# Gated DeltaNet bodies of a decoder layer: GpSimd takes six weight-tile subtractions of each body over from VectorE

## The chip, the cores and the metric

The kernel runs on one NeuronCore of a Trainium2 chip. The metric is the device time of one launch in microseconds (us), taken as the median of several runs. Engines are named PE (TensorE), DVE (VectorE), ACT (ScalarE), POOL (GpSimd) and SP (SyncE, which issues most transfers).

## What is computed

One decoder layer on 256 tokens of width 2048, in float32: a large input projection, two token mixers on its columns (a gated delta rule and a differential attention), a gated merge, an output projection with layer norm, and a SwiGLU feed-forward. Cut to what matters here:

```python
h = x @ w_in[l]                       # q, k, v, z of the delta rule, then the attention's and the gates
qkv = silu(causal_depthwise_conv(concat([q, k, v]), conv_w))
# delta rule, per head and chunk of 64 tokens:
a_mat = where(strict, einsum('cd,sd->cs', k_beta, k) * decay, 0)
sol = triangular_solve(a_mat + eye(64), [v * beta, k_beta * exp(g)], unit_diagonal=True)
...
o_a = rms_norm(o, norm_w) * silu(z)
merged = sigmoid(ga) * (o_a @ w_branch_a) + sigmoid(gb) * (o_b @ w_branch_b)
x = layer_norm(alpha * x + merged @ w_out); ffn = (silu(x @ w_gate) * (x @ w_up)) @ w_down
x = layer_norm(alpha * x + ffn)
```

## The kernel before

Every weight is read once, as a stream of 640 tiles of 128 x 1024 float32 numbers (512 KB), in the order in which they are used. A product in float32 accuracy is made from three passes in the type float32r: SP brings a tile to `raw` (a ring of four buffers), ACT rounds it to `whi` ("hi"), and the remainder `wlo = raw - whi` ("lo") is taken by a subtraction with two inputs in SBUF. PE then multiplies activations by both: 12 products of 128x512 for a tile, `act_hi*whi`, `act_hi*wlo`, `act_lo*whi`.

Order is written out by hand. The stream is cut into bodies of 32 tiles, called slots `s = 0..31` (BODY). In slot `s` PE multiplies tile `s`, while ACT (`split` on line 811) and DVE (`split` on line 1280) prepare tile `s + 3` (AHEAD = 3). Both wait for `tile_used` to reach `n + s`, so they may begin when PE has left tile `s - 1`; DVE waits for `hi_done` too. PE waits before a tile for `hi_done` and `lo_done`, which count the tiles in order (lines 440 and 441), and SP waits for both before it fills a `raw` buffer anew.

The first four bodies (j = 0 to 3, `body(0, ...)` and a loop) multiply the delta rule's k, v, q and z columns of four heads each. Between tiles the engines work at the delta rule itself, each by a list of "mixes" called after the slot's split:

- `dn_conv`: in slots 8, 10, 16, 18, 24 and 26 PE turns two heads of the projection, ACT takes the last tap, and DVE adds three others by six `SCALAR_TENSOR_TENSOR` (line 1405; one input in PSUM, one in SBUF). In the slot after, ACT applies SiLU (line 927).
- `dn_build`: the inverse of the triangular matrix. In slot 15 DVE makes masks of it (`Pm<-AT,masks`, `Tc<-Pm,masks`, `Pc<-Tc`, `Pm<-masks,Tc`). It then grows in five steps, in slots 17, 19, 20, 21 and 22 (GROW, k = 0 to 4). In each, PE waits for `dve_x`, multiplies `B<-Pm,Pc` (64 small products), and DVE makes what the next step needs:

```python
dve.wait_ge(N["pe_x"], 1 + GROWN * j + k + 1)
ch(tt(Pm[:, :, :], Pm[:, :, :], B8[1], ALU.subtract))      # one input in PSUM
ch(V.transpose(Tc[:, :, :], WT))                           # one input
tt(Pc[:, :, :], Tc[:, :, :], rep(masks[:, k + 2, :], 8), ALU.mult).then_inc(N["dve_x"], 1)   # two in SBUF
```

- `dn_scan` (slots 0 to 12 of the next body): the recurrence over chunks.

POOL has only small work in these bodies: `root` (lines 1237 to 1247), twelve instructions of 128x8 that refine a reciprocal root. Its result `rinv` is asked for in slot 13 and used in slot 28. A second root is asked for in slot 6 of the next body. Instructions on POOL and DVE run in the order in which they are written.

Of the kernel before, what the change touches and what calls it, by code (L numbers as in the profile page):

```python
# [18 lines left out]
ALU = mybir.AluOpType  # L19
# [24 lines left out]
CONV_LINKS, BUILD_LINKS, SCAN_LINKS, DA_LINKS = 12, 19, 7, 25  # L44
OT_SLOTS = (12, 14)
O_BLOCKS, V_BLOCKS = 11, 22
O_HI = 29
V_SCALED = (28, 30)
TURN = range(1, 7)
TURN_HI = 8  # L50
GAIN = (11, 13)
# [9 lines left out]
RING = 4  # L61
AHEAD = 3
# [6 lines left out]
BODY = 4 * TPG  # L69
# [32 lines left out]
def build(nc, xT, xrow, weights, w_ab, consts, early, params, lam_in, ln_in, out):  # L102
    ctx = ExitStack()

    def sb(name, shape, dt=F32):
        return ctx.enter_context(nc.sbuf_tensor(name, shape, dt))

    def sem(name):
        return ctx.enter_context(nc.semaphore(name))

    with ctx:
# [33 lines left out]
        raw = sb("raw", [P, RING, TK, NG])  # L145
        whi = sb("whi", [P, RING, TK, NG], F32R)
        wlo = sb("wlo", [P, RING, TK, NG], F32R)
# [44 lines left out]
        def conv_bank(kind, half):  # L192

            return B[1 if kind == 0 and half else 0]
# [9 lines left out]
        def d_(name):  # L204
            a, b = DS[name]
            return dsm[:, a:b]
# [48 lines left out]
        hi_done = sem("hi_done")  # L255
        lo_done = sem("lo_done")
        tile_used = sem("tile_used")
# [972 lines left out]
        @block.gpsimd  # L1230
        def _(pool):
            G = nc.gpsimd
            for n in counted:
                pool.sem_inc(N[n], 1)
            ch = Chain(pool, N["pool_chain"], 1)

            def root(o, x):

                a = half[:, 0:x.shape[1]]
                for i in range(3):  # L1240
                    ch(G.tensor_tensor(a, o, o, ALU.mult))  # L1241
                    ch(G.tensor_tensor(a, a, x, ALU.mult))
                    ch(G.tensor_scalar(a, a, -0.5, 1.5, ALU.mult, ALU.add))  # L1243
                    last = G.tensor_tensor(o, a, o, ALU.mult)
                    if i < 2:
                        ch(last)
                return last

            for j in range(NB + 1):
                if j > 0:  # L1250
                    pool.wait_ge(N["dve_qs"], 1 + j)
                    root(d_("rs"), d_("qs")).then_inc(N["pool_rs"], 1)
                if j < NB:
                    pool.wait_ge(N["dve_ss"], 1 + j + 1)
                    ch(root(d_("rk"), d_("ss")))
                    G.tensor_tensor(d_("rinv"), d_("rk"), d_("ss"), ALU.mult).then_inc(N["pool_rinv"], 1)
            for i in range(HEADS):
                pool.wait_ge(N["dve_os"], 1 + i + 1)
                root(sm[:, 48:50], sm[:, 42:44]).then_inc(N["pool_os"], 1)

        @block.vector
        def _(dve):
            V = nc.vector

            def tt(o, a, b, op):
                return V.tensor_tensor(o, a, b, op)  # L1266
# [6 lines left out]
            def stt(o, a, s, b, op0, op1):  # L1273
                return V.scalar_tensor_tensor(out=o, in0=a, scalar=s, in1=b, op0=op0, op1=op1)  # L1274
# [5 lines left out]
            def split(n, s):  # L1280

                if isinstance(n, int) and n + s + AHEAD >= N_TILES:
                    return
                r = (s + AHEAD) % RING
                dve.wait_ge(hi_done, n + s + AHEAD + 1)
                dve.wait_ge(tile_used, n + s)
                tt(wlo[:, r], raw[:, r], whi[:, r], ALU.subtract).then_inc(lo_done, 1)
# [99 lines left out]
            def dn_conv(j, s):  # L1387
                if s == 4:
                    dve.wait_ge(N["act_tap"], 1 + 6 * j)
                    a0 = PARAM["conv"][0]  # L1390
                    V.tensor_copy(cw[:, :, :, :].rearrange("p k h c -> p (k h c)").unsqueeze(1),
                                  par[:, a0:a0 + NB * 48].rearrange("p (j c) -> p j c", j=NB)
                                  [:, bass.ds(j, 1), :]).then_inc(N["dve_cw"], 1)
                for kind, slots in enumerate(CONV_SLOTS):
                    if s not in slots:
                        continue
                    half = slots.index(s)
                    link = Chain(dve, N["conv_chain"], 1 + CONV_LINKS * j + 2 * (2 * kind + half))
                    dve.wait_ge(N["act_tap"], 1 + 6 * j + 2 * kind + half + 1)
                    for back in range(1, CONV):  # L1400
                        for i in range(2):
                            h = 2 * half + i
                            w = cw[:, kind, h, CONV - 1 - back:CONV - back]
                            dst = cT[:, kind, h, back:SEQ]
                            ins = stt(dst, conv_bank(kind, half)[:, i * SEQ:(i + 1) * SEQ - back], w, dst, ALU.mult, ALU.add)
                        if back == CONV - 1:
                            ins.then_inc(N["dve_conv"], 1)
                        else:
                            link(ins)

            def v_scaled(j, t):
                tt(vr[:, t].rearrange("p h (a x) -> p h a x", x=SB), by_source(vtok).rearrange("p (h t) a x -> p h t a x", t=TOK)[:, :, t],
                   d_("rinv")[:, HB * t:HB * (t + 1)].unsqueeze(2).unsqueeze(3).broadcast_to([P, HB, 4, SB]), ALU.mult
                   ).then_inc(N["dve_v"], 1)

            def dn_build(j, s, ch):
# [54 lines left out]
                if s == V_BLOCKS:  # L1471
                    dve.wait_ge(N["act_silu"], 1 + 3 * j + 2)
                    if not isinstance(j, int):
                        dve.wait_ge(o_kept, 16 * j)
                    V.transpose(stage[:, :, :, :].rearrange("p b q x -> p q b x"),
                                cT[:, 1].rearrange("p h (q b x) -> p (h q) b x", q=TOK, x=SB)).then_inc(N["dve_vS"], 1)
                if s in V_SCALED:
                    if s == V_SCALED[0]:
                        dve.wait_ge(N["pool_rinv"], 1 + j + 1)
                        dve.wait_ge(v_full, 64 * (j + 1))  # L1480
                    v_scaled(j, V_SCALED.index(s))
                if s in (28, 29):
# [56 lines left out]
                    tt(lo(act_a, HB * j, HB, t * P, (t + 1) * P), B4[2 + t],  # L1539
                       hi(act_a, HB * j, HB, t * P, (t + 1) * P), ALU.subtract).then_inc(N["dve_oT"], 1)  # L1540

            def body(n, mixes=()):
                for s in range(BODY):
                    split(n, s)
                    for mix in mixes:
                        mix(s)

            def chained(name, base, fn, j, links, slots=BODY, **more):
                ch = Chain(dve, N[name], 1 + base)
                def run(s):  # L1550
                    fn(j, s, ch, **more)
                    if s == slots - 1:
                        assert ch.n == links, (name, ch.n)
                return run

            body(0, [prologue, chained("build_chain", 0, dn_build, 0, BUILD_LINKS), lambda s: dn_conv(0, s)])
            with dve.Fori(1, NB) as j:
                body(BODY * j, [chained("scan_chain", SCAN_LINKS * (j - 1), dn_scan, j - 1, SCAN_LINKS),
                                chained("build_chain", BUILD_LINKS * j, dn_build, j, BUILD_LINKS),
                                lambda s: dn_conv(j, s)])  # L1560

            def da_mix(j, s, ch):
                if s == 0:
# [43 lines left out]
            def da_turns(j, s, first):  # L1607
                for which, slots in enumerate(DA_TURN_FIRST if first else DA_TURN):
# [11 lines left out]
                    if i == 15:  # L1620
                        ins.then_inc(N["dve_qkT"], 1)

            body(N_DA, [chained("scan_chain", SCAN_LINKS * (NB - 1), dn_scan, NB - 1, SCAN_LINKS,
                                alone=True), lambda s: da_turns(0, s, True)])
            with dve.Fori(1, NB) as j:
# [12 lines left out]
            def turn_blocks(cnt, s, place):  # L1638

                if s == TURN[0]:  # L1640
                    dve.wait_ge(N["dve_m"], 1 + cnt + 1)
                    dve.wait_ge(N["act_mT"], 1 + 2 * cnt)
                if s in TURN:
                    at = 3 * (s - TURN[0])
                    for i in range(at, min(at + 3, 16)):
                        a, b = divmod(i, 4)
                        ins = V.transpose(blocks_out(turned)[b * SB:(b + 1) * SB, :, :, a, :],  # L1647
                                          blocks_in[a * SB:(a + 1) * SB, :, :, b, :])
                    if s == TURN[-1]:
                        ins.then_inc(N["dve_turn"], 1)  # L1650
# [28 lines left out]
            for g in range(3):  # L1679
                for q in range(TPG):  # L1680
                    s = g * TPG + q
# [304 lines left out]
```

## Time and profile before

| | |
|---|---|
| median of 3 runs | 1930.88 us (1929.91 to 1931.75) |
| the profiled execution | 1930.64 us, of it 1928.8 us from first to last instruction |
| PE busy | 1913.5 us (99%) |
| DVE busy | 1330.6 us (69%) |
| ACT busy | 928.9 us (48%) |
| POOL busy | 101.3 us (5%) |
| granted PE clock | 0.998 of full speed |

The busy times are shares of the span. PE's products overlap each other, so its 99% means that it hardly waits, not that it is at its peak.

### The profile page before, as it was taken

The page shows a single profiled execution, that of the slowest core. Times are in us where ns is not written, and L with a number is a line of the kernel's source. Part 1 is how long each engine was busy: PE and PEld are TensorE (multiplying, and loading weights), DVE is VectorE, ACT ScalarE, POOL GpSimd, SP SyncE. Part 2 cuts the span into 40 slices and gives each one's busy share as a digit, 9 for nine tenths or more (in the row PEclk, how much of TensorE's full clock was granted, in tenths as well). Part 3 has the DMA queues.
Part 4 walks back from the last instruction along what each step waited for, and adds up shares of the span by engine and source line. Part 5 has one row for each costly group of instructions (what it writes and reads, how often), then busy time and mean ns, then how long its engine had stood idle before and what let it go on. Part 6 is the DMA issues. An engine that isn't in the chain of part 4 may idle for free.

```text
span 1928.8 us, 31440 instructions
## 1 busy us (share of the span) xinstructions
PE 1913.5 (99%) x10359; PEld 1574.6 (82%) x10359; DVE 1330.6 (69%) x1872; ACT 928.9 (48%) x1308; POOL 101.3 (5%) x296
## 2 busy tenths in 40 slices
PE   9999999999999999999999999999999999999997
PEld 7788888888888888888888887888888888888886
DVE  7868688786757777776566756577675466665656
ACT  5555564554455555545544436544443444443442
POOL 0102020010002121212000000000000000000000
PEclk9999999999999999999999999999999999999999
DMA  7555555564655555555666676565666556666655
GB/s 280 165 166 184 182 172 178 167 187 146 201 171 169 179 168 179 166 182 165 206 194 191 214 248 199 175 195 189 193 196 193 191 194 191 196 192 195 196 187 175
DMA packets 103672, 362.57 MB, mean 188 GB/s; under 512 B 11472, under 2 KB 15376, under 8 KB 103440
## 3 DMA queue, kind: packets, MB, share of 16 engines
q1 hardware_dynamic: 97904, 351.65, 56.7%
q10 hardware_dynamic: 5664, 9.46, 1.5%
q8 instruction: 74, 1.21, 0.3%
q14 instruction: 30, 0.25, 0.0%
HBM read 355.28 MB, written 5.78 MB: 187 GB/s over the span
## 4 chain that ended last, share of the span: by engine, by line
PE 92%; DVE 4%; ACT 2%; issue 1%; DMA 0%; SPq 0%; DVEq 0%; ACTq 0%
PE pg L415 86%; PE B L415 4%; DVE wlo L1266 1%; DVE cT L1274 1%; DVE gates L1274 1%; DVE Pm L1266 1%; DVE AT L1266 1%; ACT QKT L959 0%; PE B L513 0%; DMA raw<-in_weights 0%; ACT whi L809 0%; PE B L666 0%; DVE Tc L1457 0%; PE B L538 0%; PE B L631 0%
## 5 line engine op out<-in xcount | busy, mean ns | idle before, releaser
L1266 DVE TENSOR_TENSOR wlo<-raw,whi 128x1024 fp32r<-128x1024 f32 (+1 forms) x640 | 779.2, 1221 | 470.0 <-ACT whi L809 452.2
L809 ACT ACTIVATE whi<-raw 128x1024 fp32r<-128x1024 f32 (+1 forms) x640 | 674.3, 1057 | 700.9 <-PE pg L415 687.1
L415 PE MATMUL pg<-whi,act_x 128*128 128x512 f32 x2960 | 950.0, 395 | 0.7 <-ACT whi L809 0.7
L415 PEld LDWEIGHTS pg<-whi,act_x 128*128 128x128 f32 x2960 | 555.5, 188 | 123.8 <-issue 7.9
L415 PE MATMUL pg<-wlo,act_x 128*128 128x512 f32 x1480 | 574.8, 390 | 0.0
L415 PE MATMUL pg<-whi,act_a 128*128 128x512 f32 x1632 | 504.9, 389 | 0.5 <-DVE act_a L1266 0.3
L415 PEld LDWEIGHTS pg<-whi,act_a 128*128 128x128 f32 x1632 | 306.3, 188 | 64.9 <-DVE act_a L1266 1.3
L415 PEld LDWEIGHTS pg<-wlo,act_x 128*128 128x128 f32 x1480 | 278.3, 188 | 53.7
L415 PE MATMUL pg<-wlo,act_a 128*128 128x512 f32 x816 | 317.5, 389 | 0.0
L415 PEld LDWEIGHTS pg<-wlo,act_a 128*128 128x128 f32 x816 | 153.2, 188 | 31.6
L415 PE MATMUL pg<-whi,act_b 128*128 128x512 f32 x512 | 158.3, 389 | 0.0
L415 PEld LDWEIGHTS pg<-whi,act_b 128*128 128x128 f32 x512 | 96.1, 188 | 19.9
L415 PE MATMUL pg<-wlo,act_b 128*128 128x512 f32 x256 | 99.6, 389 | 0.0
L1647 DVE STREAM_TRANSPOSE soft<-hraw 32x256 f32<-32x256 f32 x208 | 90.6, 436 | 3.8
L1274 DVE SCALAR_TENSOR_TENSOR cT<-B,cw,cT 128x255 f32<-128x255 f32 (+1 forms) x144 | 62.7, 477 | 5.5 <-ACT cT L922 3.6
L415 PEld LDWEIGHTS pg<-wlo,act_b 128*128 128x128 f32 x256 | 48.0, 188 | 10.1
L1073 ACT ACTIVATE soft<-soft,sm 128x128 f32<-128x128 f32 (+1 forms) x64 | 28.4, 444 | 38.2 <-DVE sm L1270 38.2
L1241 POOL TENSOR_TENSOR half<-dsm 128x8 f32<-128x8 f32 x24 | 14.3, 594 | 437.3 <-DVE dsm L1271 436.0
L900 ACT ACTIVATE hraw<-pg 128x512 f32<-128x512 f32 x40 | 21.7, 594 | 32.2 <-PE pg L415 27.4
L922 ACT ACTIVATE cT<-B,cw 128x256 f32<-128x256 f32 x48 | 20.1, 470 | 32.8 <-PE B L513 31.8
L1243 POOL TENSOR_SCALAR half<-half 128x2 f32<-128x2 f32 (+1 forms) x72 | 33.6, 467 | 6.3
L1241 POOL TENSOR_TENSOR half<-sm 128x2 f32<-128x2 f32 x48 | 11.9, 248 | 357.6 <-DVE sm L1271 355.1
(231 smaller groups left out, 1048.6 us busy)
## 6 DMA issues: line engine op xcount, KB each, us to landing
raw<-in_weights SPq DMA_DIRECT2D x646, 512.0 KB, 4.2
decm<-sums_out ACTq DMA_DIRECT2D x4, 512.0 KB, 4.4
turn_v<-stage ACTq DMA_DIRECT2D x4, 512.0 KB, 2.9
kT<-turn_v ACTq DMA_DIRECT2D x16, 128.0 KB, 2.9
gates<-in_ln_in SPq DMA_DIRECT2D x4, 512.0 KB, 6.0
gates<-in_ln_in SPq DMA_DIRECT2D x1, 2048.0 KB, 8.4
out<-gates SPq DMA_DIRECT2D x8, 256.0 KB, 2.7
turn_o<-stage ACTq DMA_DIRECT2D x3, 512.0 KB, 4.3
```

Source lines behind the costliest of these rows:

```text
L415: return nc.tensor.matmul(o, l, r, start=start, stop=stop)
L809: return nc.scalar.activation(o, i, ACT.Copy, scale=scale)
L900: last = nc.scalar.activation(dst(t), pg[pair][t][:, :], func, scale=scale)
L922: last = nc.scalar.activation(cT[:, kind, h, :], conv_bank(kind, half)[:, i * SEQ:(i + 1) * SEQ], ACT.Copy, scale=cw[:, kind, h, CONV - 1: ...
L1073: last = nc.scalar.activation(pr[:, m, a:b], pr[:, m, a:b], ACT.Exp, bias=sm[:, 28 + i:29 + i], accum_out=sm[:, 32 + i:33 + i])
L1241: ch(G.tensor_tensor(a, o, o, ALU.mult))
L1243: ch(G.tensor_scalar(a, a, -0.5, 1.5, ALU.mult, ALU.add))
L1266: return V.tensor_tensor(o, a, b, op)
L1274: return V.scalar_tensor_tensor(out=o, in0=a, scalar=s, in1=b, op0=op0, op1=op1)
L1647: ins = V.transpose(blocks_out(turned)[b * SB:(b + 1) * SB, :, :, a, :], blocks_in[a * SB:(a + 1) * SB, :, :, b, :])
```

## The change

In each delta-rule body the lo subtractions of slots 16, 18, 20, 22, 24 and 26 (those for tiles 19, 21, 23, 25, 27 and 29) are issued on POOL, behind the `rinv` of that body. Each waits for the hi of its tile, for the lo of the tile before, and for its buffer (`tile_used`). DVE leaves them out. In the slot after each it waits until POOL's lo is counted, and then goes on with the next tile's lo. The lo's of the whole stream stay in order.

```diff
+POOL_LO = (16, 18, 20, 22, 24, 26)
...
                     G.tensor_tensor(d_("rinv"), d_("rk"), d_("ss"), ALU.mult).then_inc(N["pool_rinv"], 1)
+                    for s in POOL_LO:
+                        n = BODY * j + s
+                        r = (s + AHEAD) % RING
+                        pool.wait_ge(hi_done, n + AHEAD + 1)
+                        pool.wait_ge(lo_done, n + AHEAD)
+                        pool.wait_ge(tile_used, n)
+                        G.tensor_tensor(wlo[:, r], raw[:, r], whi[:, r], ALU.subtract).then_inc(lo_done, 1)
...
-            def body(n, mixes=()):
+            def body(n, mixes=(), by_pool=()):
                 for s in range(BODY):
-                    split(n, s)
+                    if s - 1 in by_pool:
+                        dve.wait_ge(lo_done, n + s + AHEAD)
+                    if s not in by_pool:
+                        split(n, s)
                     for mix in mixes:
                         mix(s)
...
-            body(0, [prologue, chained("build_chain", 0, dn_build, 0, BUILD_LINKS), lambda s: dn_conv(0, s)])
+            body(0, [prologue, chained("build_chain", 0, dn_build, 0, BUILD_LINKS), lambda s: dn_conv(0, s)], POOL_LO)
             with dve.Fori(1, NB) as j:
...
-                                lambda s: dn_conv(j, s)])
+                                lambda s: dn_conv(j, s)], POOL_LO)
```

On POOL, between the end of a body's `rinv` (`dsm<-dsm`) and the root of the next body, there stood before:

```order
L1244 TENSOR_TENSOR dsm<-half,dsm 128x8 [waits pool_chain]
L1256 TENSOR_TENSOR dsm<-dsm 128x8 [waits pool_chain]
L1241 TENSOR_TENSOR half<-dsm 128x8 [waits dve_qs]
L1242 TENSOR_TENSOR half<-half,dsm 128x8 [waits pool_chain]
L1243 TENSOR_SCALAR half<-half 128x8 [waits pool_chain]
```

and there stands now:

```order
L1245 TENSOR_TENSOR dsm<-half,dsm 128x8 [waits pool_chain]
L1257 TENSOR_TENSOR dsm<-dsm 128x8 [waits pool_chain]
L1264 TENSOR_TENSOR wlo<-raw,whi 128x1024 [waits tile_used,lo_done,hi_done] x6
L1242 TENSOR_TENSOR half<-dsm 128x8 [waits dve_qs]
L1243 TENSOR_TENSOR half<-half,dsm 128x8 [waits pool_chain]
L1244 TENSOR_SCALAR half<-half 128x8 [waits pool_chain]
```

Six subtractions of 128x1024 have come in behind `rinv`, and nothing else on POOL has moved.

On DVE, slots 15 and 16 of the first body: the end of the mask work, the lo of slot 16, and the first of the six `cT<-B,cw,cT` of the convolution. Before:

```order
L1266 TENSOR_TENSOR Tc<-Pm,masks 128x256 [waits build_chain]
L1444 STREAM_TRANSPOSE Pc<-Tc 128x256 [waits build_chain]
L1266 TENSOR_TENSOR Pm<-masks,Tc 128x8x32
L1266 TENSOR_TENSOR wlo<-raw,whi 128x1024 [waits tile_used,hi_done,build_chain]
L1274 SCALAR_TENSOR_TENSOR cT<-B,cw,cT 128x255 [waits act_tap]
```

Now:

```order
L1274 TENSOR_TENSOR Tc<-Pm,masks 128x256 [waits build_chain]
L1452 STREAM_TRANSPOSE Pc<-Tc 128x256 [waits build_chain]
L1274 TENSOR_TENSOR Pm<-masks,Tc 128x8x32
L1282 SCALAR_TENSOR_TENSOR cT<-B,cw,cT 128x255 [waits act_tap,build_chain]
L1282 SCALAR_TENSOR_TENSOR cT<-B,cw,cT 128x255
```

The convolution now stands directly behind the mask work.

On DVE, slots 19 to 21 of the first body, with the growing steps k = 1 and k = 2 (`Pm<-Pm,B`, `Tc<-Pm`, `Pc<-Tc,masks`). Before:

```order
L1266 TENSOR_TENSOR wlo<-raw,whi 128x1024 [waits tile_used,hi_done]
L1266 TENSOR_TENSOR Pm<-Pm,B 128x512 [waits pe_x]
L1457 STREAM_TRANSPOSE Tc<-Pm 128x256 [waits build_chain]
L1266 TENSOR_TENSOR Pc<-Tc,masks 128x256 [waits build_chain]
L1266 TENSOR_TENSOR wlo<-raw,whi 128x1024 [waits tile_used,hi_done]
L1266 TENSOR_TENSOR Pm<-Pm,B 128x512 [waits pe_x]
L1457 STREAM_TRANSPOSE Tc<-Pm 128x256 [waits build_chain]
L1266 TENSOR_TENSOR Pc<-Tc,masks 128x256 [waits build_chain]
L1266 TENSOR_TENSOR wlo<-raw,whi 128x1024 [waits tile_used,hi_done]
```

Now:

```order
L1274 TENSOR_TENSOR wlo<-raw,whi 128x1024 [waits tile_used,hi_done,lo_done]
L1274 TENSOR_TENSOR Pm<-Pm,B 128x512 [waits pe_x]
L1465 STREAM_TRANSPOSE Tc<-Pm 128x256 [waits build_chain]
L1274 TENSOR_TENSOR Pc<-Tc,masks 128x256 [waits build_chain]
L1274 TENSOR_TENSOR Pm<-Pm,B 128x512 [waits pe_x]
L1465 STREAM_TRANSPOSE Tc<-Pm 128x256 [waits build_chain]
L1274 TENSOR_TENSOR Pc<-Tc,masks 128x256 [waits build_chain]
L1274 TENSOR_TENSOR wlo<-raw,whi 128x1024 [waits tile_used,hi_done,lo_done]
```

The lo between the two steps is gone from DVE, and those on either side of them wait for `lo_done` as well.

## Rows read from the trace of the kernel before

**Rows 1.** The page, part 1: busy us, share of the span, instructions.

```profile
PE 1913.5 (99%) x10359; PEld 1574.6 (82%) x10359; DVE 1330.6 (69%) x1872; ACT 928.9 (48%) x1308; POOL 101.3 (5%) x296
```

**Rows 2.** Waits of PE: total us, times, longest us.

```profile
PE B L415 <- DVE Pc L1266: 1.4, 3, 1.1
```

**Rows 3.** Line 1266, DVE's subtractions: ns of one (min/median/max), first and last start.

```profile
L1266 DVE TENSOR_TENSOR wlo<-raw,whi x640: 687/1226/1257, 4.8 to 1906.4; 128x1024 fp32r<-128x1024 f32 x159, 128x512 fp32r<-128x512 f32 x1
```

**Rows 4.** Tile dsm, the same columns.

```profile
L1244 POOL TENSOR_TENSOR dsm<-half,dsm x24: 202/203/1182, 57.3 to 486.3; 128x8 f32<-128x8 f32 x24
...
L1266 DVE TENSOR_TENSOR dsm<-dsm,cur x4: 166/167/168, 55.2 to 388.3; 128x8 f32<-128x8 f32 x4
```

**Rows 5.** Timeline, body 2, slots 14 and 15: start us, us, what.

```profile
278.02 1.23 DVE L1266 TENSOR_TENSOR wlo<-raw,whi 128x1024 fp32r<-128x1024 f32 x1
...
278.25 1.06 POOL L1242 TENSOR_TENSOR half<-half,dsm 128x8 f32<-128x8 f32 x1
...
281.73 1.27 DVE L1266 TENSOR_TENSOR AT<-B,AT 128x512 f32<-128x512 f32 x2
281.95 0.20 POOL L1242 TENSOR_TENSOR half<-half,dsm 128x8 f32<-128x8 f32 x1
```

**Rows 6.** Timeline at 626.7 us, an attention body.

```profile
626.73 0.20 POOL L1244 TENSOR_TENSOR sm<-half,sm 128x2 f32<-128x2 f32 x1
626.74 1.26 DVE L1266 TENSOR_TENSOR wlo<-raw,whi 128x1024 fp32r<-128x1024 f32 x1
```

**Rows 7.** Timeline of DVE and POOL, body 2, slots 15 to 21.

```profile
284.03 0.35 POOL L1244 TENSOR_TENSOR dsm<-half,dsm 128x8 f32<-128x8 f32 x1
284.46 0.35 POOL L1256 TENSOR_TENSOR dsm<-dsm 128x8 f32<-128x8 f32 x1
...
284.79 0.42 DVE L1266 TENSOR_TENSOR Tc<-Pm,masks 128x256 f32<-128x256 f32 x1
...
285.62 0.38 DVE L1266 TENSOR_TENSOR Pm<-masks,Tc 128x256 f32<-128x256 f32 x1
286.19 1.23 DVE L1266 TENSOR_TENSOR wlo<-raw,whi 128x1024 fp32r<-128x1024 f32 x1 [0.19 <-DVE Pm L1266]
287.33 2.68 DVE L1274 SCALAR_TENSOR_TENSOR cT<-B,cw,cT 128x255 f32<-128x255 f32 x6
289.93 1.21 DVE L1266 TENSOR_TENSOR wlo<-raw,whi 128x1024 fp32r<-128x1024 f32 x1
...
291.98 0.42 DVE L1266 TENSOR_TENSOR Pc<-Tc,masks 128x256 f32<-128x256 f32 x1
...
293.46 2.68 DVE L1274 SCALAR_TENSOR_TENSOR cT<-B,cw,cT 128x255 f32<-128x255 f32 x6
...
298.38 0.43 DVE L1266 TENSOR_TENSOR Pc<-Tc,masks 128x256 f32<-128x256 f32 x1
...
305.31 0.42 DVE L1266 TENSOR_TENSOR Pc<-Tc,masks 128x256 f32<-128x256 f32 x1
```

**Rows 8.** Timeline of ACT, body 2: hi of slots 20 and 22.

```profile
297.14 1.04 ACT L809 ACTIVATE whi<-raw 128x1024 fp32r<-128x1024 f32 x1
...
303.05 1.06 ACT L809 ACTIVATE whi<-raw 128x1024 fp32r<-128x1024 f32 x1 [3.15 <-PE pg L415]
```

**Rows 9.** Timeline of PE, body 2: growing steps k = 1, 2 and 4.

```profile
294.75 1.09 PE L415 MATMUL B<-Pm,Pc 32*32 32x64 f32 x64
...
298.96 1.10 PE L415 MATMUL B<-Pm,Pc 32*32 32x64 f32 x64
...
306.93 0.75 PE L415 MATMUL B<-Pm,Pc 32*32 32x32 f32 x64
```

**Rows 10.** Timeline of DVE and POOL, body 0, slots 15 and 16.

```profile
61.76 1.70 DVE L1266 TENSOR_TENSOR Pm<-AT,masks 32x256 f32<-32x256 f32 x4
61.80 0.44 POOL L1256 TENSOR_TENSOR dsm<-dsm 128x8 f32<-128x8 f32 x1
...
65.89 2.68 DVE L1274 SCALAR_TENSOR_TENSOR cT<-B,cw,cT 128x255 f32<-128x255 f32 x6
```

## The prediction

> **What bounds the kernel now.** I read the page first: PE is busy for 1913.5 us, 99% of the span, DVE for 1330.6, POOL for 101.3 [rows 1]. So time lies on PE's side, and relief for DVE is worth only what PE waits for DVE. The view of waits gives that directly: PE waited for the growing steps' masked tile `Pc` 3 times, 1.4 us in all, 1.1 us of it once [rows 2]. In body 2 one such wait is seen: step k = 2 starts at 298.96, 0.15 us after `Pc` ends (298.38 + 0.43 = 298.81) [rows 7, 9]. Everything else that DVE does in these bodies is hidden behind PE's tiles. The prize is at most 1.4 us, 0.07%. The rest of the question is what the change can spoil, since each us that PE waits more is a us of the kernel.
>
> **What the change removes.** Twenty-four subtractions of 1.226 us [rows 3] leave DVE, six in each of four bodies, 29.4 us of an engine that isn't the bound. Its worth is the 1.4 us above, and nothing more.
>
> **What it adds: the length of one subtraction on POOL, d.** The trace has no wide instruction on POOL. Its 128x8 `TENSOR_TENSOR` takes 0.203 us where nothing holds it up, DVE's 0.167 us [rows 4], and DVE's 128x1024 takes 1.226 us [rows 3], so DVE passes over 1016 columns in 1.06 us. The lower bound is one such pass: 0.20 + 1.06 = 1.25 us. The upper one is three passes, for two inputs and an output one after another: 0.20 + 3.18 = 3.4 us. I take two passes, 0.20 + 2.12 = 2.3 us, since the next rows speak for one common reading path for both of POOL's inputs.
>
> The Trainium skill (GPSIMD Engine Reference, section Performance versus the Vector engine) gives 4497 ns for a two-input add of 2048 columns in float32 on GpSimd; half of it is an estimate of 2.25 us. By that figure the sum below would be 0.8 us smaller. No run so far shows it.
>
> **What it adds: the two engines keep each other out.** While DVE subtracts a tile (two inputs in SBUF, 278.02 to 279.25), POOL's 128x8 instruction that began at 278.25 takes 1.06 us and ends with it; under `AT<-B,AT`, whose one input is in PSUM, the same instruction takes 0.20 us [rows 5]. The other direction shows only faintly: a subtraction that begins 0.01 us behind a POOL instruction of two columns takes 1.26 us, against the usual 1.23 [rows 6, 3]. If that is POOL's short reading, a POOL instruction of 1024 columns keeps DVE's two-input instructions out for about d. I take it so.
>
> The Trainium skill states the rule outright (SBUF — State Buffer, section Who interferes with whom): a VectorE instruction with two SBUF inputs contends with a GpSimd instruction that reads SBUF, the first to issue has the shared pair for the whole instruction, and the other is fully blocked. By this rule the change costs what follows; without it, it is worth the 1.4 us. The trace agrees for POOL as the blocked one (1.06 us); for DVE it has the 0.03 us above.
>
> What stands on DVE next to POOL's new work and has two inputs in SBUF: `Tc<-Pm,masks`, `Pm<-masks,Tc`, the lo's, and each `Pc<-Tc,masks`, for which PE waits. `Pm<-Pm,B`, the transposes and the convolution have at most one, and pass.
>
> **The path through body 2**, with d = 2.3. A time in brackets is that of before.
> - Slot 16. POOL's `rinv` ends at 284.46 + 0.35 = 284.81; `Tc` runs from 284.79 to 285.21, so POOL's first subtraction goes from 285.21 to 287.51. It keeps out `Pm<-masks,Tc` (285.62), which runs from 287.51 to 287.89. After the 0.19 us of its chain the convolution begins at 288.1 (287.33): +0.77, although the lo between them (286.19) is gone [rows 7].
> - Slots 17 and 18. The lo of slot 17 ends at 291.14 + 0.77 = 291.91. POOL waits for it and subtracts from about 291.99 to 294.29 (0.08 us as POOL's delay behind a semaphore: the instruction of 284.46 waits for the one that ends at 284.38). `Pc` of k = 0 is wanted at 291.98 + 0.77 = 292.75, waits until 294.3 and ends at 294.73. PE's step k = 1 (294.75) follows by 0.15: +0.13. The convolution of slot 18 follows `Pc` by 0.34 and begins at 294.65 (293.46): +1.19 [rows 7, 9].
> - Slots 19 and 20. Behind this convolution stand ACT's SiLU and then the hi of slot 20, which ends at 297.14 + 1.04 + 1.19 = 299.37; POOL begins at 299.45 and ends at 301.75. DVE wants `Pc` of k = 1 at 298.38 + 1.19 = 299.57. POOL is first by 0.12 us. `Pc` ends at 302.19, and PE's step k = 2 starts at 302.34 (298.96): +3.38 [rows 7, 8, 9]. This is the term that decides.
> - Slots 21 and 22. The hi of slot 22 ends at 303.05 + 1.06 + 3.38 = 307.49, and POOL runs from 307.57 to 309.87. `Pc` of k = 3, wanted at 305.31 + 3.38 = 308.69, ends at 310.3. Step k = 4 starts at 310.45 instead of 306.93 + 3.38 = 310.31: +0.14 [rows 7, 8, 9].
> - Slots 24 and 26. DVE does only convolutions and transposes beside them, and PE needs these lo's three tiles later. They cost nothing. Behind POOL's waits stands only the next body's root; behind DVE's wait for `lo_done` stand the next lo and its mixes, but POOL is done by then in each slot above. SP fills a buffer when its lo is counted, some 2 us later than before, with four tiles' time until its data are used: hidden too.
>
> Sum for the body: 3.38 + 0.14 = 3.5 us (the 0.13 is inside the 3.38). The three bodies of the loop have the same rows up to a shift.
>
> Body 0 differs at slot 16: `rinv` ends at 62.24, in the middle of the four `Pm<-AT,masks` (61.76 to 63.46), so POOL comes in behind the second of them, and the third starts 2.3 us late. Against that stands the lo that is gone (1.14 us), so the convolution (65.89) starts 1.16 us late, 0.4 more than in body 2 [rows 10]. From there the path is that of body 2: 3.9 us.
>
> **Sum.** 3 x 3.5 + 3.9 = 14.4 us. The profiled execution takes 1930.64 us, 1.8 of it outside the span, and would take 1945.1. The median of the runs is 0.2 higher (1930.88), so I forecast 1945.3 us, +0.75%.
>
> The sum is steep in d, since POOL's time enters the path in slots 16, 18 and 20 and again a little in 22: about 4 us per us of d and body, 16 in all. With d = 3.4 it is 8.1 a body, and 1963. With d = 1.25 the same walk gives `Pc` of k = 1 at 299.1 to 299.5, since the convolution of slot 18 then waits for its own taps: +0.7 a body, 1933.6.
>
> **Rivals.**
> 1. DVE wins the race in slot 20. The margin is 0.12 us; it decides if POOL needs over 0.20 us from the end of the hi to its first read. Then `Pc` ends at 300.0, k = 2 starts at 300.15 (+1.19), POOL's work falls under `Pm<-Pm,B` and the transpose, and k = 4 adds 0.15: 1.35 a body, 1.7 in body 0, 5.8 in all: 1936.7. For it: three waits stand before POOL's instruction. Against: the order shows hi_done as the one attached to the instruction itself, so the others are passed by then.
> 2. Not slower: POOL's reading doesn't keep DVE out. Mechanism and place: the two interleave during `Pc` of k = 0, 1 and 3, and nothing is late. POOL's lo of slot 20 (tile 23) is ready by about 300.6, and PE needs it at 307.6. Then the 1.4 us come in: 1929.5, within 0.2%. For it: the only sign of the lock in this direction is 0.03 us. It decides if DVE's wait is below some 1 us a body.
> 3. d is 1.6 us or less: +0.7 to +1.5 a body, 1933.6 to 1936.9. For it: POOL has the same small-instruction time as DVE within 0.04 us [rows 4].
> 4. d near three passes: 1955 to 1963.
>
> **How the numbers follow.** Forecast (both block each other, POOL first, d between 1.6 and 2.9): 0.58. Rival 1: 0.12. Rival 2: 0.15. Rival 3: 0.10, about half of it within 0.2%. Rival 4: 0.05. A measurement of this kernel tells about 0.2%, 3.9 us, from no change. Faster by more than that would need 3.9 us where PE waits for 1.4: 0.02, for something that I don't see. Same: 0.18. Slower: 0.80. The range leaves out rival 2 and the far ends of 3 and 4: 1934 to 1955. The forecast's own range is 1938 to 1954.
>
> **What would show it.** POOL's `wlo<-raw,whi` x24 at about 2.3 us each. `Pc<-Tc,masks` on DVE with a maximum near 2.7 us in place of 0.426. In the waits, PE for DVE `Pc` at about 16 us, over some 10 waits. In body 2, step k = 2 about 3.4 us later against the body's start, and slots 24 to 31 with no new gap. The forecast is wrong if `Pc` keeps its 0.43 us, if POOL's subtraction starts behind `Pc` in slot 20, or if d is far from 2.3.

## The result, and the profile after

| | before | after |
|---|---|---|
| median of the runs | 1931.1 us (1929.91 to 1931.75, 4 runs) | 1951.29 us (1950.4 to 1951.91, 4 runs) |
| ratio, with its 95% interval | | 1.0104 [1.0091, 1.0116] |
| profiled execution: time, span | 1930.64 us, 1928.8 us | 1951.3 us, 1949.5 us |
| mean granted TensorE clock | 0.998 | 0.994 |

The kernel is 20.2 us slower, 1.05%. The forecast was 1945.3 us: the sign and the range hold, the size was 14.4 us where 20.2 were measured.

The page of after, part 1, and the view of PE's waits (total us, times, longest us):

```profile
PE 1920.3 (99%) x10359; PEld 1579.4 (81%) x10359; DVE 1330.7 (68%) x1848; ACT 928.3 (48%) x1308; POOL 158.5 (8%) x320
```

```profile
PE B L416 <- DVE Pc L1274: 13.7, 7, 3.3
PE B L416 <- DVE TTf L1304: 1.5, 1, 1.5
PE B L416 <- DVE Pc L1452: 1.0, 1, 1.0
```

Twenty-four instructions have left DVE, and yet its busy time is the same to 0.1 us [rows 1]: most of the 29.4 us that went came back as longer instructions, held up while they were already counted as busy. (In e4 below, where POOL does the same 24 subtractions and holds up none of DVE's two-input instructions, DVE is busy for 1303.4 us, 27.2 less.) The wait of PE for `Pc` has gone from 1.4 us [rows 2] to 14.7 (13.7 and 1.0). PE is also *busy* for 6.8 us longer with the same 10359 instructions, which no wait explains.

The new POOL line and the line of `Pc` in after (ns of one: min/median/max, first and last start):

```profile
L1264 POOL TENSOR_TENSOR wlo<-raw,whi x24: 2339/2398/2667, 62.5 to 452.0; 128x1024 fp32r<-128x1024 f32 x24
L1274 DVE TENSOR_TENSOR Pc<-Tc,masks x16: 424/1790/2499, 71.8 to 436.6; 128x256 f32<-128x256 f32 x16
```

POOL takes 2.4 us for a tile against DVE's 1.23 [rows 3], and a `Pc` that took 0.42 us before [rows 7] takes up to 2.50. Body 2 shows how, in the timeline of DVE, POOL and ACT (start us, us, what, and in brackets an idle time ahead and what ended it):

```profile
296.64 2.40 POOL L1264 TENSOR_TENSOR wlo<-raw,whi 128x1024 fp32r<-128x1024 f32 x1
296.65 2.67 DVE L1274 TENSOR_TENSOR Tc<-Pm,masks 128x256 f32<-128x256 f32 x1
...
304.18 2.40 POOL L1264 TENSOR_TENSOR wlo<-raw,whi 128x1024 fp32r<-128x1024 f32 x1 [5.15 <-DVE wlo L1274]
304.89 1.98 DVE L1274 TENSOR_TENSOR Pc<-Tc,masks 128x256 f32<-128x256 f32 x1
306.79 2.67 DVE L1282 SCALAR_TENSOR_TENSOR cT<-B,cw,cT 128x255 f32<-128x255 f32 x6
...
310.46 1.99 ACT L810 ACTIVATE whi<-raw 128x1024 fp32r<-128x1024 f32 x2
311.58 2.34 POOL L1264 TENSOR_TENSOR wlo<-raw,whi 128x1024 fp32r<-128x1024 f32 x1 [5.00 <-ACT whi L810]
311.71 2.50 DVE L1274 TENSOR_TENSOR Pc<-Tc,masks 128x256 f32<-128x256 f32 x1
...
316.71 0.42 DVE L1274 TENSOR_TENSOR Pc<-Tc,masks 128x256 f32<-128x256 f32 x1
...
319.58 2.40 POOL L1264 TENSOR_TENSOR wlo<-raw,whi 128x1024 fp32r<-128x1024 f32 x1 [5.66 <-ACT whi L810]
320.71 1.56 DVE L1274 TENSOR_TENSOR Pc<-Tc,masks 128x256 f32<-128x256 f32 x1
```

Each DVE instruction here with both inputs in SBUF ends 0.28 to 0.29 us behind the end of POOL's subtraction (299.04 and 299.32; 306.58 and 306.87; 313.92 and 314.21; 321.98 and 322.27), however early it began. It is 0.28 to 0.29 us for all sixteen such pairs of the four bodies. The one `Pc` under which POOL does nothing (316.71) keeps its 0.42 us. The pair that decides is that of slot 20, POOL at 311.58 and DVE at 311.71: POOL is first by 0.13 us, and by 0.12 or 0.13 us in the three other bodies.

The growing steps of PE, in the timeline of PE: k = 2 of body 1 with products behind it, then k = 1 to 4 of body 2 with products behind k = 2:

```profile
198.41 1.10 PE L416 MATMUL B<-Pm,Pc 32*32 32x64 f32 x64 [3.27 <-DVE Pc L1274]
...
200.04 1.05 PE L416 MATMUL pg<-whi,act_x 128*128 128x512 f32 x2
200.89 0.63 PE L416 MATMUL pg<-wlo,act_x 128*128 128x512 f32 x1
201.32 1.05 PE L416 MATMUL pg<-whi,act_x 128*128 128x512 f32 x2
...
307.02 1.10 PE L416 MATMUL B<-Pm,Pc 32*32 32x64 f32 x64 [0.17 <-DVE Pc L1274]
314.36 1.09 PE L416 MATMUL B<-Pm,Pc 32*32 32x64 f32 x64 [3.30 <-DVE Pc L1274]
...
315.95 0.63 PE L416 MATMUL pg<-whi,act_x 128*128 128x512 f32 x2
316.42 0.39 PE L416 MATMUL pg<-wlo,act_x 128*128 128x512 f32 x1
316.64 0.63 PE L416 MATMUL pg<-whi,act_x 128*128 128x512 f32 x2
...
318.34 1.10 PE L416 MATMUL B<-Pm,Pc 32*32 32x64 f32 x64
...
322.42 0.74 PE L416 MATMUL B<-Pm,Pc 32*32 32x32 f32 x64
```

Before, steps k = 1, 2 and 4 started at 294.75, 298.96 and 306.93 [rows 9]. They are now 12.27, 15.40 and 15.49 us later. The body itself comes 11.86 us later (the end of `rinv`, 284.81 before, 296.67 now), so within it the shift is 0.41, 3.54 and 3.63 us. The jump stands at k = 2, where PE pauses 3.30 us.

**The clock.** Four stretches behind that pause, one in each body, in the view of windows (window, its us, busy us of PE, PEld, DVE, ACT and POOL with their instructions, PEclk, DMA share, GB/s):

```profile
81.20:87.80 6.60, 6.53 (x76) 5.32 (x76) 2.69 (x4) 0.00 (x0) 0.00 (x0) 0.54 0.35 98
199.40:203.90 4.50, 4.50 (x19) 3.31 (x12) 2.69 (x4) 0.00 (x0) 0.00 (x0) 0.62 0.41 122
315.40:318.30 2.90, 2.90 (x16) 2.15 (x12) 2.69 (x4) 0.00 (x0) 0.00 (x0) 1.00 0.42 162
428.70:434.20 5.50, 5.46 (x76) 4.38 (x76) 2.70 (x4) 0.00 (x0) 0.00 (x0) 0.70 0.28 98
```

PE is busy throughout, but in bodies 0, 1 and 3 the granted clock is 0.54, 0.62 and 0.70 over the stretch, that is 1.2 GHz for part of it and 2.4 for the rest; in body 2 it is 2.4 throughout. The products show it in the timeline above: three of them (two with `whi`, one with `wlo`) go from 200.04 to 201.32 in body 1, 1.28 us, and from 315.95 to 316.64 in body 2, 0.69 us. What it costs I took from start times: the same product of PE is found in both traces, and its shift is read ahead of the slow stretch and behind it. The shift grows there by 2.76 us in body 0, 1.58 in body 1, nothing in body 2, 1.48 in body 3, 5.8 us in all. (The windows give a bound: if everything in them went by the clock, 6.60 x 0.46 + 4.50 x 0.38 + 5.50 x 0.30 = 6.4 us.) The rest of the shift is waiting, 3.6 us in every body, 14.4 in all. 14.4 + 5.8 = 20.2 of the 20.7 us by which the span grew; of the 0.5 us that are left, 0.3 stand in PE's start times already at 12 us, ahead of the first changed slot, and the rest isn't placed.

### The profile page after: what moved, and what is told of

The parts are those of the page before. It is cut to its first block, busy times and chain, and to the rows that moved or that the text cites. A ratio compares the mean times of both kernels' runs of the same rounds, so it can differ in the third digit from the quotient of the medians.

```text
span 1949.5 us, 31441 instructions
## 1 busy us (share of the span) xinstructions
PE 1920.3 (99%) x10359; PEld 1579.4 (81%) x10359; DVE 1330.7 (68%) x1848; ACT 928.3 (48%) x1308; POOL 158.5 (8%) x320
## 4 chain that ended last, share of the span: by engine, by line
PE 91%; DVE 5%; ACT 2%; issue 1%; DMA 0%; SPq 0%; DVEq 0%; ACTq 0%
PE pg L416 85%; PE B L416 4%; DVE wlo L1274 1%; DVE cT L1282 1%; DVE Pm L1274 1%; DVE Pc L1274 1%; DVE gates L1282 1%; DVE AT L1274 1%; DVE Tc L1274 0%; ACT QKT L960 0%; ACT whi L810 0%; DMA raw<-in_weights 0%; PE B L514 0%; PE B L667 0%; ACT hraw L1149 0%
## 5 line engine op out<-in xcount | busy, mean ns | idle before, releaser
L1274 DVE TENSOR_TENSOR wlo<-raw,whi 128x1024 fp32r<-128x1024 f32 (+1 forms) x616 | 750.2, 1220 | 465.5 <-ACT whi L810 448.5
L1264 POOL TENSOR_TENSOR wlo<-raw,whi 128x1024 fp32r<-128x1024 f32 x24 | 57.6, 2399 | 116.8 <-ACT whi L810 73.6
L416 PEld LDWEIGHTS B<-Pm,Pc 32*32 32x32 f32 x1408 | 20.6, 111 | 23.5 <-issue 23.5
L416 PE MATMUL B<-Pm,Pc 32*32 32x64 f32 (+1 forms) x1408 | 23.5, 214 | 15.1 <-DVE Pc L1274 13.7
```

The lines of the kernel that those rows point to most:

```text
L416: return nc.tensor.matmul(o, l, r, start=start, stop=stop)
L1264: G.tensor_tensor(wlo[:, r], raw[:, r], whi[:, r], ALU.subtract).then_inc(lo_done, 1)
```

## The experiments

The kernel before was timed anew beside each group of experiments: its median is 1930.85 us beside e1 to e4, 1930.6 beside e5 to e8, and 1930.74 beside e9 and e10. A pause, a start time or a profile line below is of the profiled execution; "Measured" is the median of all runs.

### Two of the six, where DVE has nothing waiting behind: e1

```diff
-POOL_LO = (16, 18, 20, 22, 24, 26)
+POOL_LO = (24, 26)
```

> Only the lo's of slots 24 and 26 go to POOL, beside which DVE has convolutions and transposes (one input in SBUF at most). Theory (POOL's reading keeps DVE's two-input instructions out, and PE waits for the late Pc): nothing late, 1931 us within 2 us, and no half-speed stretch of PE. Rival (the handing over itself costs, by DVE's wait for POOL's lo and later refills): a third of the 14.4 us of waits, about +5 us.

Measured: 1931.15 us, ratio 1.0001 [0.9992, 1.0011]. PE waits for `Pc` 1.3 us, twice; `Pc` takes 0.424 to 0.427 us; POOL's eight subtractions take 2.39 us on the mean. The 9.8 us taken off DVE (eight subtractions) are worth nothing here, and POOL's work costs nothing where no instruction with two inputs in SBUF is due on DVE beside it.

### Slot 20 alone: e2, and all but slot 20: e3

```diff
-POOL_LO = (16, 18, 20, 22, 24, 26)
+POOL_LO = (20,)
```

> Only the lo of slot 20 goes to POOL. Theory: the hi of slot 20 is ready 0.2 us before DVE wants Pc of k = 1 (before: 298.18 against 298.38 us in body 2), so POOL is first and Pc ends about 2.3 us late: +2.3 us a body, 9.2 us in all, 1940.3 us, plus what PE loses at half clock if it falls there. Pc of k = 1 about 2.6 us long on DVE. Rival (a sum of small delays of all six slots, or DVE is first): under +3 us.

Measured: 1943.72 us (1940.82 to 1946.25, 4 runs), ratio 1.007 [1.0054, 1.0085]. In e2's waits, and in the line of `Pc`:

```profile
PE B L416 <- DVE Pc L1274: 9.9, 4, 3.1
```

```profile
L1274 DVE TENSOR_TENSOR Pc<-Tc,masks x16: 424/426/2515, 70.6 to 427.1; 128x256 f32<-128x256 f32 x16
```

One subtraction in each body is enough for a wait in each body: the pause at k = 2 is 3.15 us in body 0 and 2.25 in the three others, 2.1 us a body more than before (8.3 in all by start times, where 9.2 were expected). Behind the pause of body 0 the clock falls again, in e2's windows:

```profile
82.00:85.00 3.00, 3.00 (x8) 2.32 (x8) 2.33 (x4) 0.00 (x0) 0.00 (x0) 0.50 0.04 14
```

That cost 2.6 us in the profiled execution (1941.49 us: 8.3 + 2.6 = 10.9 on a span 10.9 longer). The kernel's four runs are the widest of the study, and they go with the mean granted clock: 1940.82 at 0.997, 1941.49 at 0.996, 1945.96 at 0.995, 1946.25 at 0.994. Only the second of them has a trace. With the same instructions in all four, their mean clocks say that they spent more or less time at the low clock; after which pauses the other three did isn't recorded.

```diff
-POOL_LO = (16, 18, 20, 22, 24, 26)
+POOL_LO = (16, 18, 22, 24, 26)
```

> The change without slot 20. Theory: Pc of k = 0 and 3 are still kept out, the convolution of slot 18 comes 1.2 us late and with it Pc of k = 1, but that one is not kept out: +1.35 us in bodies 1 to 3 and 1.7 in body 0, about +5.8 us, 1937 us. PE's pauses stay under 2 us, and if the half-speed stretches come of the 3.3 us pauses, there is none here. Rival (half speed has nothing to do with the pauses): stretches of 0.43 us products remain.

Measured: 1937.06 us, ratio 1.0032 [1.002, 1.0044], clock 0.998 in every run. In e3's waits:

```profile
PE B L416 <- DVE Pc L1274: 5.4, 7, 1.2
```

With 1.0 us for the first `Pc` that is 6.4 us, 5.0 more than before. By the same view e2's waits are 8.5 us more than before (9.9 - 1.4). Together they make 13.5 us, against the 13.3 that the whole change added (14.7 - 1.4): the two parts nearly add up. Without slot 20 no pause for `Pc` is over 1.22 us, and the clock stays up.

### The same six, POOL behind DVE's short instruction: e4 and e10

The kernel after, with POOL's subtraction of slot 16 behind the mask work and those of slots 18, 20 and 22 behind the `Pc` that they had kept out.

```diff
+POOL_BEHIND = {18: 2, 20: 3, 22: 5}
...
                         pool.wait_ge(tile_used, n)
+                        if s == 16:
+                            pool.wait_ge(N["build_chain"], 1 + BUILD_LINKS * j + 8)
+                        if s in POOL_BEHIND:
+                            pool.wait_ge(N["dve_x"], 1 + GROWN * j + POOL_BEHIND[s])
```

> All six lo's on POOL, but POOL also waits until DVE's two-input work of the slot is done: behind the masks in slot 16, behind Pc of k = 0, 1 and 3 in slots 18, 20 and 22. Theory (the port order is all): nothing of DVE's is kept out but the lo's, PE's 1.4 us of waits are gone, 1929 to 1931 us. Rival (two engines in turn on one stream of lo's cost by themselves, or POOL's 2.4 us falls on something else): above 1935 us.

Measured: 1929.22 us (1928.53 to 1930.22, 11 runs), ratio 0.9993 [0.9984, 1.0002]. The view of waits has no row of PE for `Pc` any more. The line of `Pc` in e4:

```profile
L1279 DVE TENSOR_TENSOR Pc<-Tc,masks x16: 424/426/426, 69.5 to 414.5; 128x256 f32<-128x256 f32 x16
```

and slot 20 of body 2 in e4's timeline:

```profile
296.63 0.42 DVE L1279 TENSOR_TENSOR Pc<-Tc,masks 128x256 f32<-128x256 f32 x1
297.22 2.38 POOL L1269 TENSOR_TENSOR wlo<-raw,whi 128x1024 fp32r<-128x1024 f32 x1 [4.66 <-DVE Pc L1279]
```

POOL does all 24 subtractions at the same 2.38 us, 0.17 us behind `Pc` instead of 0.13 us ahead of it, and the 20.2 us are gone. The prize shows in the trace too: the shift of PE's products against before falls by 1.14 us at k = 2 of body 0 and by 0.22 to 0.24 us there in each other body, and the span is 1.7 us shorter.

> The version with POOL behind the two-input work of each slot once more, to narrow its interval. Its trace had lost 1.65 us of PE's waits in four places and nothing else. Theory: 1.4 to 1.7 us under the kernel before, ratio 0.9992. Rival: no difference, and the first measurement was chance.

The same kernel again: 1929.22 us (1928.6 to 1929.91, 11 runs), ratio 0.9992 [0.9983, 1.0001]. Twice 0.08% below, and each interval just takes in 1. The trace shows the waits gone; the times can't quite tell it from no change.

### The order in slot 20 alone: e9

```diff
+POOL_BEHIND = {20: 3}
...
                         pool.wait_ge(tile_used, n)
+                        if s in POOL_BEHIND:
+                            pool.wait_ge(N["dve_x"], 1 + GROWN * j + POOL_BEHIND[s])
```

> The change, in which only POOL's lo of slot 20 also waits for Pc of k = 1; slots 16, 18 and 22 stay as they are. Theory (in slot 20 the order of the two instructions is the whole 2 us a body): as with slot 20 left out, +1.35 us in bodies 1 to 3 and 1.7 in body 0, 1937 us, at full clock. Rival (it is that slot 20 is done by POOL at all): as the change, 1951 us.

Measured: 1936.87 us, ratio 1.0032 [1.002, 1.0044], clock 0.998. In e9's waits:

```profile
PE B L417 <- DVE Pc L1277: 5.4, 7, 1.2
```

The same row as e3's, and the same time within 0.2 us: it makes no measured difference whether POOL does slot 20's subtraction or DVE, if POOL starts behind `Pc`. Turning this one pair round leaves 6.1 us over before (1936.87 against 1930.74) of the 20.2; they are slots 16, 18 and 22, since slots 24 and 26 cost nothing in e1.

### POOL idle, DVE late by itself: e5 and e6

The kernel before, with dummy subtractions on DVE between the transpose and `Pc` of k = 1, so that PE pauses at k = 2 while POOL does nothing. Three in a chain, and one. The computation is untouched.

```diff
                         ch(V.transpose(Tc[:, :, :], WT))
+                        if k == 1:
+                            for i in range(3):
+                                tt(soft[:, 0:8 * P], cst[:, 0:8 * P], cst[:, 0:8 * P], ALU.subtract).then_inc(N["pause"], 1)
+                                dve.wait_ge(N["pause"], 1 + 3 * j + i + 1)
                         tt(Pc[:, :, :], Tc[:, :, :], rep(masks[:, k + 2, :], 8), ALU.mult).then_inc(N["dve_x"], 1)
```

> The kernel before, with three idle subtractions of 128x1024 on DVE between the transpose and Pc of k = 1, chained, about 1.4 us each; POOL has no new work. PE then waits some 4.2 us more at step k = 2 of each body (16.8 us in all). Theory (after the 3.3 us pauses PE ran at 1.2 GHz for a while, and that was the 5.8 us beyond the waits): half-speed products behind these pauses too, so more than 16.8 us, by 1.5 to 3 us a body: 1953 to 1960 us. Rival (the half speed came of POOL's work or of reading conflicts): 16.8 us and full clock, 1948 us.

Measured: 1952.58 us, ratio 1.0115 [1.0098, 1.0132], clock 0.994. In e5's waits and windows:

```profile
PE B L415 <- DVE Pc L1266: 16.8, 4, 4.9
```

```profile
197.60:200.00 2.40, 2.39 (x65) 2.20 (x66) 1.40 (x2) 0.00 (x0) 0.00 (x0) 0.50 0.17 26
313.50:316.00 2.50, 2.45 (x65) 2.22 (x66) 1.50 (x2) 0.00 (x0) 0.00 (x0) 0.50 0.20 41
```

Pauses of 4.86, 4.07, 3.92 and 3.92 us, and behind every one of them PE runs at 1.2 GHz at once. By start times the waits cost 15.2 us, where 16.8 were expected, and the clock 5.7 (1.38 to 1.48 a body), so the time is just under the expected 1953 to 1960. POOL's column is zero: a pause of PE brings the low clock without any work of POOL.

```diff
                         ch(V.transpose(Tc[:, :, :], WT))
+                        if k == 1:
+                            for _ in range(1):
+                                tt(soft[:, 0:8 * P], cst[:, 0:8 * P], cst[:, 0:8 * P], ALU.subtract)
```

> The same with one idle subtraction: PE waits about 1.2 us more at step k = 2 of each body, 4.8 us in all. Theory: so short a pause is followed by full clock: 1936 us. Rival (any pause there lowers the clock): some 6 us more.

Measured: 1936.99 us, ratio 1.0033 [1.002, 1.0045], clock 0.998. In e6's windows:

```profile
80.00:83.00 3.00, 3.00 (x19) 2.27 (x12) 2.59 (x4) 0.00 (x0) 0.00 (x0) 0.58 0.51 175
193.00:196.00 3.00, 3.00 (x46) 2.48 (x35) 2.77 (x5) 0.00 (x0) 0.00 (x0) 1.00 0.45 143
```

Pauses of 2.21 us in body 0 and 1.57, 1.29 and 1.30 in the others. Only behind that of body 0 is the clock low (1.57 us more); the waits cost 4.8 us. The expected full clock came behind three of the four pauses, and the 2.21 us of the fourth weren't short enough.

### POOL busy beside the kernel before, with two inputs and with none: e7 and e8

The kernel before, with a dummy on POOL behind the hi of slot 20, first a subtraction of 128x1024 (both of its inputs are the same tile), then three fills of the same size.

```diff
+                    pool.wait_ge(hi_done, BODY * j + 20 + AHEAD + 1)
+                    ch(G.tensor_tensor(soft[:, 0:8 * P], cst[:, 0:8 * P], cst[:, 0:8 * P], ALU.subtract))
```

> The kernel before, DVE does all its lo's; POOL does one idle subtraction of 128x1024 with two inputs in SBUF in each body, as soon as the hi of slot 20 is there. Theory (reading keeps DVE out): Pc of k = 1 is 2.6 us long, +2.3 us a body, 9.2 in all, plus half-clock time if it falls there: 1940 us or more. Rival (the cost of slot 20 is DVE's waiting for POOL's lo, or the lo itself being late): no change, 1931 us.

Measured: 1939.23 us (1938.27 to 1940.71, 4 runs), ratio 1.0047 [1.003, 1.0064]. In e7's waits, and its timeline in body 2:

```profile
PE B L415 <- DVE Pc L1268: 8.1, 4, 2.7
```

```profile
302.63 1.90 POOL L1258 TENSOR_TENSOR soft<-cst 128x1024 f32<-128x1024 f32 x1 [13.46 <-ACT whi L809]
302.75 2.05 DVE L1268 TENSOR_TENSOR Pc<-Tc,masks 128x256 f32<-128x256 f32 x1
```

```diff
+                    pool.wait_ge(hi_done, BODY * j + 20 + AHEAD + 1)
+                    for _ in range(3):
+                        ch(G.memset(soft[:, 0:8 * P], 0.0))
```

> As the run before it, but POOL does three memsets of 128x1024 in place of the subtraction: it is busy at the same place for 2 us or more, and reads nothing. Theory (only POOL's reading keeps DVE out): no change, 1931 us, Pc stays at 0.43 us. Rival (any work of POOL at that place holds DVE up): as with the subtraction, +9 us.

Measured: 1930.78 us, ratio 1.0001 [0.9991, 1.0011]. In e8's timeline in body 2:

```profile
298.33 2.97 POOL L1259 MEMSET soft<- 128x1024 f32 x3 [13.43 <-ACT whi L809]
298.47 0.43 DVE L1269 TENSOR_TENSOR Pc<-Tc,masks 128x256 f32<-128x256 f32 x1
```

Nothing is taken off DVE in e7, neither DVE nor PE waits for the dummy, and still `Pc` takes 2.05 us and each body is 1.6 us longer by start times. The dummy was shorter than the real subtraction (1.90 us against 2.4), and so the cost is below the expected 2.3. The four bodies make 6.4 of the 7.7 us by which the profiled execution is longer; 1.1 us stand in its first 12 us, ahead of the first dummy, and no run explains these. Two of the other runs, at 1940.1 and 1940.7 us, have a mean clock of 0.997 and 0.996, the profiled one 0.998. In e8 POOL is at work for even longer, its first fill begins 0.14 us ahead of the same `Pc`, but it only writes, and `Pc` has its 0.43 us. So what keeps the two-input instruction out is a POOL instruction that *reads* SBUF, not POOL's being busy, nor the waits on `lo_done` that the change adds on DVE. A POOL instruction with a single input was not tried.

## Why the prediction was right, and where it was too small

**The bound and the prize: right.** In e1 less work on DVE was worth nothing. e4 and e10 come out 1.5 to 1.6 us below before, which fits the 1.4 us but which the timing can't tell from none; their traces show the waits gone.

**The length d: right.** 2.3 us forecast, 2.34 to 2.41 in the trace (2.67 once, in body 0, where it began under DVE's mask work). The choice of two passes between bounds of one and three rested on an argument, and came out. The estimate of 2.25 us from the Trainium skill (GPSIMD Engine Reference, section Performance versus the Vector engine) was 0.09 to 0.16 us short.

**Both keep each other out: right,** and rival 2 is gone. In the direction of which the trace of before had only 0.03 us to show, after has `Pc` at 2.50 us and `Tc` at 2.67, and e7 against e8 separates it from all else. The Trainium skill (SBUF — State Buffer, section Who interferes with whom) says this outright, that GpSimd's reads contend and its mere writes don't; both halves hold here, with 2.05 us for `Pc` in e7 and 0.43 in e8.

**The race in slot 20: right.** POOL first by 0.12 to 0.13 us in all four bodies where 0.12 was worked out, and it decides the size: e9 turns it round, and 14.1 of the 20.2 us go. Rival 1's sum was 5.8 us for the four bodies; e9, where DVE is first, gives 6.1.

**The walk of a body: right in sum, one step wrong.** 3.6 us a body against 3.5, and 14.4 us of waits against 14.4. In slot 16 I let `Tc` run ahead of POOL; in the trace POOL is first by 0.01 us (296.64 and 296.65), and it is `Tc`, not `Pm<-masks,Tc`, that takes 2.67 us. Also an instruction that was kept out ends 0.28 to 0.29 us behind POOL's end, not a full 0.42. Step k = 1 of body 2 came 0.41 us late within the body where 0.13 was worked out, k = 2 3.54 where it was 3.38, and k = 4 3.63 where it was 3.52. By the prediction's own slope of 4 us per us of d, the 0.1 us by which d was too small would add 0.4 us a body, and the shorter ends of some 0.14 us in four places take about as much away. That the waits agree to the tenth is luck. Body 0 was to cost 0.4 us more than the others; by start times its waits cost the same 3.6. Slots 24 and 26 cost nothing, as forecast (e1). (One figure beside the walk is off: with d = 3.4 it gives 7.9 us a body, not 8.1; the 1963 us beside it fits 7.9.)

**The wait view: nearly.** 14.7 us over 8 waits, where I said about 16 over some 10.

**What failed: a term was missing, not mis-sized. The sum had none for PE's clock behind the new pause.** "Each us that PE waits more is a us of the kernel" was the step, and it holds only as long as the clock stays where it was. It is 5.8 us of the 20.2: 2.76, 1.58, 0 and 1.48 us in the four bodies. e5 shows that a pause is enough to bring it (POOL idle, each of the four pauses of 3.92 us or more followed by 1.2 GHz), and e3 and e9 that without the long pause the clock stays at 0.998. Nothing in the rows of before could have given the size: PE had no pause of over 1.1 us for `Pc` there.

**What stays open: when a pause of middle length costs the clock.** All pauses at k = 2, sorted by length, with the clock behind them:

| pause, us | where | clock behind it |
|---|---|---|
| 3.92 to 4.86, four of them | e5 | 1.2 GHz |
| 3.30 | after, body 2 | 2.4 GHz |
| 3.26 to 3.29, three | after, bodies 0, 1, 3 | 1.2 GHz |
| 3.15 | e2, body 0 | 1.2 GHz |
| 2.70 | e7, body 0 | 2.4 GHz |
| 2.25, three | e2, bodies 1 to 3 | 2.4 GHz |
| 2.21 | e6, body 0 | 1.2 GHz |
| 1.79 and less, six | e7, e6, bodies 1 to 3 | 2.4 GHz |
| 1.22 and less | e3, e9, all bodies; before, e1, e8 | 2.4 GHz |

The length alone doesn't decide: 3.30 and 2.70 us are followed by the high clock, 2.21 by the low one. e2's runs differ among themselves by 5.4 us with the same instructions. The Trainium skill (TensorE: Matmul & The Clock Gate, section Part 1: The HAM clock gate) says that the chip judges the array's activity on a beat that doesn't start with the kernel, so that the same kernel can come out differently; this scatter agrees, but no run here shows the beat. For the next forecast these runs give a term with a range: between nothing and some 2.8 us behind each long pause.

## What to carry to other kernels

Moving elementwise work from an engine that isn't the bound to an idle one is worth only the waits for the first; here 1.4 us of 29.4. On GpSimd the work cost about twice the time here (2.4 us against 1.23), and in each pair where GpSimd was first a VectorE instruction with two inputs in SBUF took until 0.28 us behind its end: so look up what VectorE wants in that time and who waits for it, and start GpSimd *behind* the short instruction that PE waits for (four lines of waits made 1951 us into 1929 here). Where an edit puts a pause of some us into a PE that was hardly ever idle, add a term for a low clock behind it, and expect its size to vary: here none to 2.8 us for each.

## What the runs showed of the hardware

- POOL began 0.12 to 0.13 us ahead of DVE's `Pc` in slot 20 of all four bodies. By the start times of after and e9 this order alone puts step k = 2 2.1 us later.
- POOL's subtraction of 128x1024 takes 2.34 to 2.41 us with two different inputs and output in fp32r, and 1.90 us with the same tile as both inputs and output in float32 (e7). Which of the two differences makes it shorter was not tried.
- POOL's fill of 128x1024 takes 0.95 us (2.97 for three with the gaps between them) and did not lengthen DVE's two-input instruction (e8).
- Behind a pause of 2.2 to 4.9 us the granted clock of PE was at 1.2 GHz for long enough to cost 1.4 to 2.8 us in nine of fourteen cases, and not at all in the others.
